# Two slots of query projection added ahead of a recurrence that keeps its slot number

## Chip, cores and metric

The kernel runs on one core of a Trainium2 chip. The metric is the device time of one execution in microseconds (us), the median of three runs. The core has five engines that run side by side, each through its own queue of instructions: TensorE (PE, matmuls, into the eight banks of PSUM), VectorE (DVE), ScalarE (ACT), GpSimd (POOL) and SyncE (SP, here the issuer of DMAs). They wait for one another by semaphores.

## What is computed

One step of a small streaming encoder layer in fp32, on 512 prompt tokens and 64 sample tokens (576 in all, 1024 wide). The part of the reference that the change touches:

```python
h = rmsnorm(x, norm1_g)
proj = h @ w_in
qa, ka, va, qb, fb, ib, gb = jnp.split(proj, [o1, o2, o3, o4, o5, o6], axis=-1)
att, k_new, v_new = swa_sink_attention(qa, ka, va, k_hist, v_hist, pos0, attn_sink)   # chunks of 64 queries
rec, s_new = hgrn2(qb, fb, ib, gb, lb, hgrn_norm_g, s0)
...
# hgrn2: per chunk, cum = cumsum(log f)
q_in = qf * jnp.exp(cum - ref);  k_in = kf * jnp.exp(ref - cum)
a = tril(q_in @ k_in.T);  o_intra = a @ vf
ds = (kf * jnp.exp(tot - cum)).T @ vf
...
o = (o_intra + o_inter), normed * norm_g * silu(g_in)
x = x + jnp.concatenate([att, rec], axis=-1) @ w_o
x = x + hier_moe(rmsnorm(x, norm2_g), ...);  final rmsnorm
```

The history of keys and the recurrent state are given for the sample tokens and zero for the prompt.

## The kernel before

Every engine's program is written out by hand in one function, with hand-placed semaphore waits. Tokens are cut into five tiles (four of 128, tile 4 with 64 rows), and chunks of 64 for the attention (NCHUNK = 9). fp32 products are made of three matmuls each over a high part and a low remainder of both operands; for weights, `high` (ACT) and `low` (DVE) make the two parts, and `splits` says in which slot. For tile 4 of the kinds f, i and g a projection (`halved`) packs the high and low part of the 64 tokens into one stationary operand, so it has 16 matmuls in place of 24; its two halves are added by `add_half` on DVE after ACT copied one of them.

The list `groups` gives the order of projections on PE: f (5 tiles), k and v (2 halves of the tokens each), q (4 head groups by 2 halves of 288 tokens), and then the fillers: i (5), b (8 halves, the recurrence's query), g (5: tile 4 first, then 0 to 3). Projection n writes PSUM bank n % 2 and waits till projection n - 2 has been emptied from it by `empty` on ACT or DVE.

After the first `first_filler` projections each engine walks over `slots`. In slot s PE makes the fill projections of the slot, then `scores(s)`, `turn_p(s - 1)` (transposes of the softmax) and `attend(s - 2)`; DVE makes `softmax_tail(s - 1)`, the emptying of the fill (or `add_half`), `softmax_head(s)`, `pt_with(s - 1)`, `take_o(s - 2)`; ACT makes the exponentials. POOL places q of a chunk into the block-diagonal operand `qbd`. The first step of the recurrence (tile 0) is tied to the slots by the constant EARLY = NCHUNK + 2 = 11: in slot 11 PE makes `decays(0)`, ACT `cum_exps(0)`, DVE a memset, the copies of k for the output (kout), `operands(0)` and `gain(0)` (which multiplies g of tile 0 by the norm's gain), and PE, behind the fill, `inner(0)`; in slot 12 DVE makes `inner_and_states(0)`, whose first operation is a masked copy of the scores, then `gain(1)`, and PE, behind the fill, `sums(0)`; in slot 13 DVE makes `normed(0)`. There are 14 slots, numbered from 0. The rest (recurrence of tiles 1 to 4 with the output projection w_o, router, experts) follows.

In the f stage x tiles are transposed by `turn_x(t)`, split by `h_high` (ACT) and `h_low` (DVE), and the squares for the norm are summed by `first_squares` on ACT.

Of the kernel before, what the change touches and what calls it, by code (L numbers as in the profile page):

```python
# [32 lines left out]
D = 1024  # L33
KC = D // P
# [4 lines left out]
CHUNK = 64  # L39
# [54 lines left out]
def program(nc, io):  # L94
    ctx = ExitStack()
    with ctx:
# [133 lines left out]
        oml = lb_bc[:, BW:2 * BW]  # L230
        kf_flat = kf[:, :, :].rearrange("p t k -> p (t k)")
        lb_t = kf_flat[:, 2 * BW:4 * BW]
        junk = kf_flat[:, 0:D]
        hT_flat = hT_f[:, :, :].rearrange("p k t -> p (k t)")
        s_flat = s_buf[:, :, :, :].rearrange("p a m k -> p (a m k)")
        vT = s_flat[:, 0:TOK]
        pt_flat = pt[:, 0, :, :].rearrange("p b k -> p (b k)")

        def hgrn_buffers(t):
# [128 lines left out]
            groups.append(("f", t, "act"))  # L368
        groups += [("k", 0, "dve"), ("k", 1, "dve")]
        groups += [("v", 0, "act"), ("v", 1, "act")]  # L370
        groups += [("q", i, "dve") for i in range(2 * GROUP)]
        first_filler = len(groups)
        groups += [("i", t, "act") for t in range(NT)]
        groups += [("b", i, "dve") for i in range(2 * BH)]
        groups += [("g", t, "act") for t in (NT - 1, 0, 1, 2, 3)]
# [11 lines left out]
        def wait_emptied(eng, kinds):  # L387

            for who, s in (("act", proj_act), ("dve", proj_dve)):
# [2 lines left out]
                    eng.wait_ge(s, max(last))  # L392


        slots = [[n] for n in of_kind["i"]] + [of_kind["b"][2 * m:2 * m + 2] for m in range(BH)] + \
                [[n] for n in of_kind["g"]]
        assert len(slots) >= NCHUNK + 2

# [31 lines left out]
        def h_lo(c):  # L430
            return (hT_lo_a, hT_lo_b)[c // (KC // 2)][:, c % (KC // 2), :]


        splits = {1: (4, 0, 4), 2: (4, 4, KC), 6: (5, 0, 4), 7: (5, 4, KC),

                  EARLY: (len(W_GROUPS), 0, 3), EARLY + 1: (len(W_GROUPS), 3, 6)}

        halved = [n for n, (kind, t, _) in enumerate(groups) if kind in "fig" and t == NT - 1]
        assert rows_of(NT - 1) == DEC and 2 * DEC == P
# [169 lines left out]
        def _(pool):  # L609
# [82 lines left out]
                      allow_small_or_imprecise_dtypes=True).then_inc(consts, 1)  # L692


            wait_emptied(pool, "q")
            for c in range(NCHUNK):
                if c >= 2:
                    pool.wait_ge(scores_ready, c - 1)
                for b in range(KV):
                    rows = slice(b * HD, (b + 1) * HD)  # L700
                    pool.tensor_copy(qbd[rows, c % 2, :, b * CHUNK:(b + 1) * CHUNK],  # L701
                                     qa[rows, :, c * CHUNK:(c + 1) * CHUNK]).then_inc(qbd_ready, 1)

                    pool.wait_ge(qbd_ready, KV * c + b + 1)
# [80 lines left out]
        def _(act):  # L785
# [63 lines left out]
            high(0, 4, KC)  # L849
            h_high(1)  # L850
            first_squares(1)
            h_high(2)
            first_squares(2)
            first_squares(3)
            act.wait_ge(lb_diff, 1)
            act.activation(lb_t[:, :], lb_t[:, :], ACT.Exp).then_inc(lb_exp, 1)
            first_squares(4)
            for n in range(first_filler):
                if groups[n][2] == "act":
                    empty(n)  # L860
                kind, index, _ = groups[n]
                if kind == "f" and index < 2:
                    h_high(3 + index)
                if (kind, index) == ("f", 2):
                    high(1, 0, KC)
                if kind == "v":
                    high(2, index * KC // 2, (index + 1) * KC // 2)
                if (kind, index) == ("q", 1):
                    act.wait_ge(v_turned, 1)
                    for tile in range(PROMPT_TILES):  # L870
                        act.activation(V[:, tile, :], ps[:, 7, tile * P:(tile + 1) * P], ACT.Copy,
                                       scale=stats[:, 3, tile:tile + 1]).then_inc(v_ready, 1)
                    act.activation(V[0:DEC, 5, :], ps[0:DEC, 6, 0:KVW], ACT.Copy,
                                   scale=stats[0:DEC, 3, NT - 1:NT]).then_inc(v_ready, 1)
                if (kind, index) == ("q", 5):
                    high(3, 0, KC)
                if groups[n][0] == "k" and groups[n][1] == 1:
                    for t in range(NT):
                        act.wait_ge(f_ready, t + 1)
                        act.activation(logf[0:rows_of(t), t, :], logf[0:rows_of(t), t, :], ACT.Ln).then_inc(logf_ready, 1)  # L880
# [39 lines left out]
                last.then_inc(osq_ready, 1)  # L920

            for s, fill in enumerate(slots):
                if s == NCHUNK:

                    wait_emptied(act, "b")
                    act.activation(qf[:, :, :], qf[:, :, :], ACT.Silu).then_inc(qf_ready, 1)
                if s == EARLY:
                    cum_exps(0)
                if s == EARLY + 2:
                    rec_squares(0)  # L930
                for n in fill:
                    if groups[n][2] == "act":
                        empty(n)
                if has_before(s - 1) and s - 1 < NCHUNK:
                    pt_before(s - 1)
                if s < NCHUNK:
                    exps(s)
                if s in splits:
                    high(*splits[s])
# [130 lines left out]
        def _(dve):  # L1070
# [321 lines left out]
            for s, fill in enumerate(slots):  # L1392
                if s == EARLY + 1:
                    inner_and_states(0)
                    gain(1)
                if s == EARLY + 2:
                    normed(0)
                if 1 <= s <= NCHUNK:
                    softmax_tail(s - 1)
                for n in fill:  # L1400
                    if groups[n][2] == "dve":
                        empty(n)
                    elif n in halved:
                        add_half(n)
                if s < NCHUNK:
                    softmax_head(s)
                if 1 <= s <= NCHUNK:
                    pt_with(s - 1)
                if 2 <= s < NCHUNK + 2:
                    take_o(s - 2)  # L1410
                if s == EARLY:
                    chain(dve.memset(hgrn_buffers(0)[3], 0.0))
                    dve.wait_ge(kout_turned, 1)
                    chain(dve.tensor_copy(kout[:, 0, :], ps[:, 6, 0:P]))
                    dve.tensor_copy(kout[0:DEC, 1, :], ps[0:DEC, 6, P:2 * P]).then_inc(kout_ready, 1)
                    operands(0)
                    gain(0)
                if s in splits:
                    low(*splits[s])
            chain(dve.memset(logits[:, :, :], 0.0))  # L1420
            def mix_low(t):
# [253 lines left out]
        def _(pe):  # L1675
# [8 lines left out]
                                        ident[0:r, 0:r])  # L1684
                last.then_inc(turned, 1)

            def project(n):

                kind, i, _ = groups[n]
                k = ring_of[kind]  # L1690
# [4 lines left out]
                b = n % 2  # L1695
                hi, lo = w_hi[k % RING], w_low(k)
                for c in range(KC):
                    if fresh:

                        pe.wait_ge(w_lo_done, KC * k + c + 1)  # L1700
                    if kind in "fig":
                        cols = slice(0, 512)
                        h_parts = (hT_hi[:, c, tok(i)], h_lo(c)[:, tok(i)])
                        w_parts = (hi[:, c, cols], lo[:, c, cols])
                        out = ps[0:rows_of(i), b, 0:cols.stop - cols.start]
                        stationary, moving = h_parts, w_parts
                    else:
                        m, half = ("kv".index(kind), i) if kind in "kv" else (i // 2, i % 2)
                        cols, toks = slice(m * P, (m + 1) * P), slice(half * HALF, (half + 1) * HALF)
                        stationary = (hi[:, c, cols], lo[:, c, cols])  # L1710
                        moving = (hT_hi[:, c, toks], h_lo(c)[:, toks])
                        out = bank(b, HALF)

                    if n in halved:
                        if c:
                            pe.matmul(out, hT_both[:, c, 0:DEC], moving[1], start=False, stop=False)
                        last = pe.matmul(ps[:, b, :], hT_both[:, c, :], moving[0], start=c == 0, stop=c == KC - 1)
                        if c == 0:
                            pe.matmul(out, hT_both[:, c, 0:DEC], moving[1], start=False, stop=False)
                        continue  # L1720
                    pe.matmul(out, stationary[0], moving[0], start=c == 0, stop=False)  # L1721
                    pe.matmul(out, stationary[0], moving[1], start=False, stop=False)  # L1722
                    last = pe.matmul(out, stationary[1], moving[0], start=False, stop=c == KC - 1)  # L1723
# [11 lines left out]
            stay_busy(8)  # L1735
            for t in range(NT):
                pe.wait_ge(hT_dve, t + 1)
                project(t)
                for following in ((1, 2), (3,), (4,), (), ())[t]:
                    turn_x(following)  # L1740

            pe.wait_ge(ck_in, 16)
            pe.wait_ge(hT_dve, NT)
# [146 lines left out]
            for s, fill in enumerate(slots):  # L1890
                if s == EARLY:

                    pe.wait_ge(o_taken, NCHUNK)
                    pe.transpose(ps[:, 6, 0:P], kT[:, SEQ - P:SEQ], ident[:, :])
                    pe.transpose(ps[0:DEC, 6, P:2 * P], kT[:, SEQ + WINDOW:], ident[:, :]).then_inc(kout_turned, 1)
                    decays(0)
                for n in fill:
                    project(n)
                if s < NCHUNK:
# [233 lines left out]
```

## Time and profile before

| | us |
|---|---|
| median of 3 runs | 532.94 (532.36 to 533.3) |
| the profiled execution, its own time | 531.83 |
| its span (first to last instruction) | 530.0 |
| PE busy | 477.0 (90%) |
| DVE busy | 335.2 (63%) |
| ACT busy | 231.0 (44%) |
| POOL busy | 104.8 (20%) |

The profile is of one execution. Busy shares are over the whole span; the stages have different limits. Times of rows are us from the start of the span.

### The profile page before, as it was taken

The numbers are of one execution on the slowest core, as the hardware profiler recorded it, in microseconds if no ns is written. First come the engines' busy times: TensorE is split into PE (matmuls) and PEld (weight loads), VectorE is DVE, ScalarE is ACT, GpSimd is POOL, SyncE is SP. The second block draws the span as 40 slices with busy tenths as digits, with TensorE's granted clock in tenths as the row PEclk, the third lists the DMA queues.
The fourth block names the chain that finished last, engine by engine and source line by source line (L and its number), as shares of the span: only waits on it lengthen the run. The fifth ranks groups of instructions, "written<-read, shape, count | busy, mean of one in ns | idle before, by whom it ended". The sixth has DMA issues, their size and how long they took to land.

```text
span 530.0 us, 7159 instructions
## 1 busy us (share of the span) xinstructions
PE 477.0 (90%) x2531; PEld 376.2 (71%) x2531; DVE 335.2 (63%) x659; ACT 231.0 (44%) x446; POOL 104.8 (20%) x168
## 2 busy tenths in 40 slices
PE   6899999899999999999998988899999999999400
PEld 5679898778896777678876877666766776677100
DVE  4786515676586357767563649697568657765176
ACT  6744712453355447224132234467266456544021
POOL 5481001101000000001001044021322322222143
PEclk9999999989999999999999868899999999999855
DMA  8804404004008500610110776999989989801295
GB/s 307 190 2 160 167 0 160 0 1 160 1 1 219 166 1 9 171 41 0 41 61 1 293 302 242 420 394 374 358 345 369 376 357 350 357 16 36 66 328 187
DMA packets 33100, 93.15 MB, mean 176 GB/s; under 512 B 10248, under 2 KB 13456, under 8 KB 26928
## 3 DMA queue, kind: packets, MB, share of 16 engines
q1 hardware_dynamic: 27728, 82.81, 43.3%
q0 software_dynamic: 5344, 9.97, 5.2%
q8 instruction: 17, 0.28, 0.2%
q14 instruction: 11, 0.09, 0.1%
HBM read 88.38 MB, written 13.89 MB: 193 GB/s over the span
## 4 chain that ended last, share of the span: by engine, by line
PE 75%; DVE 13%; ACT 5%; DMA 4%; issue 2%; SPq 1%; POOL 1%; POOLq 0%; ACTq 0%; DVEq 0%
PE ps L2053 10%; PE ps L1721 7%; PE ps L1723 6%; PE ps L1722 6%; PE ps L2072 6%; PE ps L2074 5%; PE ps L2073 5%; PE ps L1935 3%; PE ps L1937 3%; PE ps L1936 3%; DMA pair<-y_pairs 2%; PE ps L1959 2%; DVE gu_lo L1588 2%; DVE w_lo L1105 2%; PE ps L2034 2%
## 5 line engine op out<-in xcount | busy, mean ns | idle before, releaser
L1588 DVE TENSOR_TENSOR gu_lo<-we_gu,gu_hi 128x1024 fp32r<-128x1024 f32 x64 | 74.8, 1220 | 2.0 <-ACT gu_hi L1003 0.6
L1003 ACT ACTIVATE gu_hi<-we_gu 128x1024 fp32r<-128x1024 f32 x64 | 63.2, 1055 | 0.0
L2053 PE MATMUL ps<-we_d,hhT 128*128 128x512 f32 x128 | 56.9, 592 | 0.0
L2072 PE MATMUL ps<-gu_hi,xT_hi 128*128 128x512 f32 x128 | 52.9, 413 | 3.4 <-DVE xT_lo L1582 3.3
L2074 PE MATMUL ps<-gu_hi,xT_lo 128*128 128x512 f32 x128 | 50.9, 397 | 0.0
L2073 PE MATMUL ps<-gu_lo,xT_hi 128*128 128x512 f32 x128 | 50.4, 394 | 0.0
L1721 PE MATMUL ps<-hT_hi,w_hi 128*128 128x288 f32 x160 | 48.3, 302 | 0.6 <-DVE w_lo_q L1102 0.2
L1721 PE MATMUL ps<-w_hi,hT_hi 128*128 128x512 f32 x96 | 39.8, 414 | 2.4 <-DVE hT_lo_b L1088 1.1
L2053 PEld LDWEIGHTS ps<-we_d,hhT 128*128 128x128 f32 x128 | 23.4, 191 | 24.9 <-issue 24.9
L1722 PE MATMUL ps<-w_lo,hT_hi 128*128 128x512 f32 x96 | 38.0, 396 | 0.0
L1048 ACT ACTIVATE sg<-ps 128x256 f32<-128x256 f32 x16 | 6.1, 383 | 64.7 <-PE ps L2074 64.7
L1624 DVE TENSOR_TENSOR hh<-sg,ps 128x256 f32<-128x256 f32 x16 | 6.7, 421 | 41.3 <-ACT sg L1048 41.2
L1721 PEld LDWEIGHTS ps<-hT_hi,w_hi 128*128 128x128 f32 x160 | 30.1, 188 | 3.3 <-DVE w_lo_q L1102 1.7
L2072 PEld LDWEIGHTS ps<-gu_hi,xT_hi 128*128 128x128 f32 x128 | 24.5, 192 | 9.4 <-issue 2.5
L732 POOL DMA_INDIRECT y_pairs<-y,now_pair x12 | 13.9, 1162 | 79.8 <-DVE y L1617 78.0
L1105 DVE SCALAR_TENSOR_TENSOR w_lo<-ring,g_col,w_hi 128x512 fp32r<-128x512 f32 (+1 forms) x40 | 25.3, 697 | 7.0 <-ACT w_hi L815 7.0
L815 ACT ACTIVATE w_hi<-ring,g_col 128x512 fp32r<-128x512 f32 (+1 forms) x48 | 28.7, 681 | 0.6 <-DMA ring<-in_w_in 0.6
L1723 PE MATMUL ps<-hT_hi,w_lo 128*128 128x288 f32 x96 | 28.3, 295 | 0.0
L2073 PEld LDWEIGHTS ps<-gu_lo,xT_hi 128*128 128x128 f32 x128 | 24.5, 192 | 5.2 <-issue 0.5
L2074 PEld LDWEIGHTS ps<-gu_hi,xT_lo 128*128 128x128 f32 x128 | 24.3, 190 | 5.5
L701 POOL COPY qbd<-qa 64x256 f32<-64x256 f32 x18 | 7.2, 400 | 93.3 <-PE ps L1769 47.7
L1936 PE MATMUL ps<-w_lo,mix_hi 128*128 128x512 f32 x64 | 25.0, 390 | 0.0
(386 smaller groups left out, 1123.6 us busy)
## 6 DMA issues: line engine op xcount, KB each, us to landing
we_gu<-in_w_gate SPq DMA_DIRECT2D x16, 1024.0 KB, 7.8
we_gu<-in_w_up SPq DMA_DIRECT2D x16, 1024.0 KB, 11.1
we_d<-in_w_down SPq DMA_DIRECT2D x16, 1024.0 KB, 11.0
ring<-in_w_in SPq DMA_DIRECT2D x4, 2048.0 KB, 7.7
pair<-y_pairs SPq DMA_DIRECT2D x8, 512.0 KB, 7.8
ring<-in_w_in SPq DMA_DIRECT2D x3, 1024.0 KB, 8.0
x_first<-in_x_p SPq DMA_DIRECT2D x4, 512.0 KB, 9.6
x<-in_x_p SPq DMA_DIRECT2D x4, 512.0 KB, 4.0
```

The costliest lines, as they stand in the source:

```text
L815: act.activation(w_split(k, w_high(k, c)), w_raw(k, c), ACT.Copy, scale=gain).then_inc(w_hi_done, 1)
L1003: act.activation(gu_hi[slot % 2][:, :, 2 * q:2 * q + 2, :], we_gu[slot][:, :, 2 * q:2 * q + 2, :], ACT.Copy).then_inc(gu_hi_done, 1)
L1105: ins = dve.scalar_tensor_tensor(out, w_raw(k, c), g1_col[:, c:c + 1], hi, ALU.mult, ALU.subtract)
L1588: dve.tensor_tensor(gu_lo[slot][:, :, 2 * q:2 * q + 2, :], we_gu[slot][:, :, 2 * q:2 * q + 2, :], gu_hi[slot % 2][:, :, 2 * q:2 * q + 2, : ...
L1721: pe.matmul(out, stationary[0], moving[0], start=c == 0, stop=False)
L1722: pe.matmul(out, stationary[0], moving[1], start=False, stop=False)
L1723: last = pe.matmul(out, stationary[1], moving[0], start=False, stop=c == KC - 1)
L1936: pe.matmul(out, mix_hi[:, c, 0:r], w_l, start=False, stop=False)
L2053: last = pe.matmul(bank(4 + 2 * (slot % 2) + half), hhT[:, slot % 2, f, :], we_d[slot][:, f, 512 * half:512 * half + 512], start=f == 0, s ...
L2072: pe.matmul(bank(0), xT_hi[:, c, :], gu_h[:, :, c, :], start=c == 0, stop=False)
L2073: pe.matmul(bank(0), xT_hi[:, c, :], gu_l[:, :, c, :], start=False, stop=False)
L2074: last = pe.matmul(bank(0), xT_lo[:, c, :], gu_h[:, :, c, :], start=False, stop=c == KC - 1)
```

## The change

The second halves of the four q groups become fillers and form two new slots ahead of the others, so there are 16 slots: q, q, i x5, b x4 (two projections each), g x5. EARLY stays 11, so all five g are now in slots 11 to 15. Moved with them: the weight splits of slots 1, 2, 6, 7 go to 3, 4, 7, 8 with the low parts one slot later, behind `softmax_tail`; those of w_o go from EARLY, EARLY + 1 to EARLY + 2, EARLY + 3; the Silu of the recurrence's query moves from slot 9 to slot 10. POOL begins with chunk 0 when the first q halves are emptied. The x transposes stand inside the f projections, and the scratch of the squares (`junk`) moves to `s_buf`. `decays(0)` goes ahead of the wait for the last attention output and of the kout transposes.

```diff
@@ tables @@
-        groups += [("q", i, "dve") for i in range(2 * GROUP)]
+        groups += [("q", 2 * m, "dve") for m in range(GROUP)]
         first_filler = len(groups)
+        groups += [("q", 2 * m + 1, "dve") for m in range(GROUP)]
         groups += [("i", t, "act") for t in range(NT)]
...
-        slots = [[n] for n in of_kind["i"]] + [of_kind["b"][2 * m:2 * m + 2] for m in range(BH)] + \
+        late_q = of_kind["q"][GROUP:]
+        slots = [late_q[0:2], late_q[2:4]] + [[n] for n in of_kind["i"]] + [of_kind["b"][2 * m:2 * m + 2] for m in range(BH)] + \
                 [[n] for n in of_kind["g"]]
...
-        splits = {1: (4, 0, 4), 2: (4, 4, KC), 6: (5, 0, 4), 7: (5, 4, KC),
+        splits = {3: (4, 0, 4), 4: (4, 4, KC), 7: (5, 0, 4), 8: (5, 4, KC),
...
-                  EARLY: (len(W_GROUPS), 0, 3), EARLY + 1: (len(W_GROUPS), 3, 6)}
+                  EARLY + 2: (len(W_GROUPS), 0, 3), EARLY + 3: (len(W_GROUPS), 3, 6)}
@@ POOL @@
-            wait_emptied(pool, "q")
             for c in range(NCHUNK):
+                if c == 0:
+                    pool.wait_ge(proj_dve, emptied[of_kind["q"][GROUP - 1]][1])
+                if c == HALF // CHUNK:
+                    wait_emptied(pool, "q")
@@ ACT @@
             h_high(1)
             first_squares(1)
-            h_high(2)
             first_squares(2)
-            first_squares(3)
             act.wait_ge(lb_diff, 1)
             act.activation(lb_t[:, :], lb_t[:, :], ACT.Exp).then_inc(lb_exp, 1)
-            first_squares(4)
+            h_high(2)
...
                     h_high(3 + index)
+                    first_squares(3 + index)
...
-                if s == NCHUNK:
+                if s == EARLY - 1:
@@ DVE @@
                 if 1 <= s <= NCHUNK:
                     softmax_tail(s - 1)
+                    if s - 1 in splits:
+                        low(*splits[s - 1])
...
-                if s in splits:
+                if s in splits and s >= EARLY:
                     low(*splits[s])
@@ PE @@
-            def project(n):
+            def project(n, following=None):
...
+                    if c == (2 if n else 5) and following is not None:
+                        turn_x(following)
...
-                project(t)
-                for following in ((1, 2), (3,), (4,), (), ())[t]:
-                    turn_x(following)
+                project(t, t + 1 if t < NT - 1 else None)
...
+                    decays(0)
                     pe.wait_ge(o_taken, NCHUNK)
                     pe.transpose(ps[:, 6, 0:P], kT[:, SEQ - P:SEQ], ident[:, :])
                     pe.transpose(ps[0:DEC, 6, P:2 * P], kT[:, SEQ + WINDOW:], ident[:, :]).then_inc(kout_turned, 1)
-                    decays(0)
```

The order of instructions shows it at three places. First DVE at the first slots that split weights, before (line L1105 makes the low parts, L1213 to L1216 are the softmax tail of chunk 1, L1198 the next softmax head):

```order
L1205 TENSOR_TENSOR small<-sink_bc,small 128x4
L1225 COPY pt<-ps 64x512
L1105 SCALAR_TENSOR_TENSOR w_lo_105<-ring,g_col,w_hi_86 128x512 x4
L1213 TENSOR_TENSOR small<-small 128x4
L1214 RECIPROCAL small<-small 128x4
L1216 TENSOR_SCALAR s_buf<-s_buf,small 128x128 x4
L1198 TENSOR_TENSOR s_buf<-ps,bias 128x4x192
```

and after, where DVE first splits weights in a slot (the same lines are L1109, L1217 to L1220 and L1202 there):

```order
L1229 COPY pt<-ps 64x512
L1233 COPY mixT<-ps 128x4x64
L1217 TENSOR_TENSOR small<-small 128x4
L1218 RECIPROCAL small<-small 128x4
L1220 TENSOR_SCALAR s_buf<-s_buf,small 128x192 x4
L1109 SCALAR_TENSOR_TENSOR w_lo_105<-ring,g_col,w_hi_86 128x512 x4
L1202 TENSOR_TENSOR s_buf<-ps,bias 128x4x192
```

The low parts stood ahead of a softmax tail and now stand behind one, three chunks later.

Second, DVE in slots 9 to 12, before (the row of gg with 64 rows is `add_half` of g's tile 4; L1412 to L1415 are memset and kout copies, L1247 to L1257 `operands(0)`, L1238 `gain`, L1277 the masked copy):

```order
L1133 TENSOR_TENSOR gg<-gg,ps 64x512
L1225 COPY pt<-ps 64x512
L1229 COPY mixT<-ps 128x4x64 x2
L1412 MEMSET pt 128x512
L1414 COPY kout<-ps 128x128
...
L1247 TENSOR_TENSOR s_buf<-s_buf,qf 128x512
L1249 TENSOR_TENSOR s_buf<-s_buf,ps 128x512
...
L1238 TENSOR_TENSOR gg<-gg,ng_bc 128x512
L1107 TENSOR_TENSOR w_lo_105<-ring,wo_hi_top 128x512 x2
L1107 TENSOR_TENSOR w_lo_105<-ring,wo_hi_q 128x512
L1277 COPY_PREDICATED pt<-causal,ps 128x512
```

and after, from slot 10 on:

```order
L1229 COPY pt<-ps 64x512
...
L1233 COPY mixT<-ps 128x4x64
L1137 TENSOR_TENSOR gg<-gg,ps 64x512
L1418 MEMSET pt 128x512
L1420 COPY kout<-ps 128x128
...
L1251 TENSOR_TENSOR s_buf<-s_buf,qf 128x512
L1253 TENSOR_TENSOR s_buf<-s_buf,ps 128x512
...
L1242 TENSOR_TENSOR gg<-gg,ng_bc 128x512
L1281 COPY_PREDICATED pt<-causal,ps 128x512
```

The addition of the half tile moved from ahead of the last attention copies to directly ahead of the memset, and between gain(0) and the masked copy no weights are split.

Third, PE from the last attention matmuls to `inner(0)`, before (L1894 and L1895 are the kout transposes, L1827 to L1834 the decays, L1721 to L1723 a full projection of 24 matmuls, L1851 the start of `inner(0)`):

```order
L1809 MATMUL ps<-pt,V 64x256 x2
L1894 MATMUL ps<-ident,kT 128x128
L1895 MATMUL ps<-ident,kT 64x128
L1827 MATMUL ps<-decay_m,logf 128x256
L1832 MATMUL ps<-ident,kf 128x128
...
L1834 MATMUL ps<-logf,tail_m 128x512
L1721 MATMUL ps<-w_hi_87,hT_hi 128x512
L1722 MATMUL ps<-w_lo_106,hT_hi 128x512
...
L1723 MATMUL ps<-w_hi_87,hT_lo_b 128x512
L1851 MATMUL ps<-s_buf 128x128 x4
```

and after (L1724 to L1727 are the halved projection of 16 matmuls):

```order
L1815 MATMUL ps<-pt,V 64x256 x2
L1833 MATMUL ps<-decay_m,logf 128x256
L1838 MATMUL ps<-ident,kf 128x128
...
L1840 MATMUL ps<-logf,tail_m 128x512
L1901 MATMUL ps<-ident,kT 128x128
L1902 MATMUL ps<-ident,kT 64x128
L1725 MATMUL ps<-w_hi_87,hT_both 128x512
L1727 MATMUL ps<-w_lo_106,hT_both 64x512
...
L1725 MATMUL ps<-w_hi_87,hT_both 128x512
L1857 MATMUL ps<-s_buf 128x128 x4
```

The decays come first, and the projection between them and `inner(0)` is the halved one.

## Rows read from the trace of the kernel before

**Rows 1.** The page: busy us and share of the span; chain by engine.

```profile
PE 477.0 (90%) x2531; PEld 376.2 (71%) x2531; DVE 335.2 (63%) x659; ACT 231.0 (44%) x446; POOL 104.8 (20%) x168
...
PE 75%; DVE 13%; ACT 5%; DMA 4%; issue 2%; SPq 1%; POOL 1%; POOLq 0%; ACTq 0%; DVEq 0%
```

**Rows 2.** Timeline, PE, f projections: start, us, line, count, [idle before, releaser].

```profile
18.15 0.50 PE L1721 MATMUL ps<-w_hi,hT_hi 128*128 128x512 f32 x1 [1.14 <-DVE hT_lo_b L1088]
...
23.77 1.04 PE L1683 MATMUL ps<-ident,x_first 128*128 128x128 f32 x8
25.68 0.47 PE L1721 MATMUL ps<-w_hi,hT_hi 128*128 128x512 f32 x1 [0.87 <-ACT logf L836]
```

**Rows 3.** Timeline, DVE, ACT and PE, end of f and second half of k.

```profile
43.83 0.67 DVE L1133 TENSOR_TENSOR logf<-logf,ps 64x512 f32<-64x512 f32 x1
...
44.53 0.72 ACT L830 ACTIVATE logf<-logf,stats 64x512 f32<-64x512 f32 x1 [2.53 <-DVE logf L1133]
...
45.88 0.29 PE L1721 MATMUL ps<-hT_hi,w_hi 128*128 128x288 f32 x1
```

**Rows 4.** Timeline, DVE and PE, third slot.

```profile
100.70 2.74 DVE L1105 SCALAR_TENSOR_TENSOR w_lo<-ring,g_col,w_hi 128x512 fp32r<-128x512 f32 x4 [1.84 <-ACT w_hi L815]
...
104.84 0.66 PE L1785 MATMUL ps<-ident,s_buf 128*128 128x128 f32 x4 [1.39 <-DVE s_buf L1216]
```

**Rows 5.** Windows, PE: stretch, its us, PE busy, granted clock, DMA share, GB/s.

```profile
105.00:107.00 2.00, 2.00 (x12) 0.91 0.03 8
107.00:110.00 3.00, 3.00 (x9) 0.50 0.00 0
...
308.00:321.00 13.00, 13.00 (x64) 0.50 0.52 201
...
324.00:326.00 2.00, 0.23 (x3) 1.00 0.93 287
...
332.00:334.00 2.00, 0.70 (x7) 1.00 1.02 422
...
335.00:338.00 3.00, 3.00 (x9) 0.56 1.01 418
```

**Rows 6.** Timeline, PE, from slot 9 to inner(0).

```profile
167.98 0.65 PE L1806 MATMUL ps<-pt,V 64*64 64x256 f32 x4
...
176.57 0.33 PE L1894 MATMUL ps<-ident,kT 128*128 128x128 f32 x1 [0.53 <-DVE mixT L1229]
...
185.37 1.05 PE L1851 MATMUL ps<-s_buf 128*128 128x128 f32 x8
```

**Rows 7.** Timeline, DVE, slots 9 to 12.

```profile
169.54 0.68 DVE L1133 TENSOR_TENSOR gg<-gg,ps 64x512 f32<-64x512 f32 x1 [2.63 <-ACT gg L827]
170.14 0.68 DVE L1225 COPY pt<-ps 64x512 f32<-64x512 f32 x1
...
176.57 0.48 DVE L1412 MEMSET pt<- 128x512 f32 x1
...
177.44 0.28 DVE L1415 COPY kout<-ps 64x128 f32<-64x128 f32 x1
180.72 0.69 DVE L1247 TENSOR_TENSOR s_buf<-s_buf,qf 128x512 f32<-128x512 f32 x1 [2.99 <-ACT s_buf L906]
...
182.73 0.68 DVE L1257 TENSOR_TENSOR s_buf<-s_buf,kf 128x512 f32<-128x512 f32 x1
...
188.62 0.73 DVE L1277 COPY_PREDICATED pt<-causal,ps 128x512 f32<-128x512 int32 x1
```

**Rows 8.** Timeline, ACT, slots 9 to 11.

```profile
168.91 0.59 ACT L827 ACTIVATE gg<-ps 64x512 f32<-64x512 f32 x1
...
185.57 0.69 ACT L842 ACTIVATE gg<-ps,stats 128x512 f32<-128x512 f32 x1 [2.11 <-PE ps L1723]
```

**Rows 9.** Timeline, PE, first and last matmul of g's half tile, slot 9.

```profile
162.84 0.51 PE L1717 MATMUL ps<-w_hi,hT_both 128*128 128x512 f32 x1
...
166.42 0.40 PE L1717 MATMUL ps<-w_hi,hT_both 128*128 128x512 f32 x1
```

More of the change, by code:

```diff
@@ L232, in program @@
         lb_t = kf_flat[:, 2 * BW:4 * BW]
-        junk = kf_flat[:, 0:D]
         hT_flat = hT_f[:, :, :].rearrange("p k t -> p (k t)")
@@ L236, in program @@
         vT = s_flat[:, 0:TOK]
+        junk = s_flat[:, 0:D]
         pt_flat = pt[:, 0, :, :].rearrange("p b k -> p (b k)")
@@ L867, in _ @@
                     high(2, index * KC // 2, (index + 1) * KC // 2)
-                if (kind, index) == ("q", 1):
+                if (kind, index) == ("q", 2):
                     act.wait_ge(v_turned, 1)
@@ L874, in _ @@
                                    scale=stats[0:DEC, 3, NT - 1:NT]).then_inc(v_ready, 1)
-                if (kind, index) == ("q", 5):
+                if (kind, index) == ("q", 4):
                     high(3, 0, KC)
```

## The prediction, before the changed kernel ran

> **What bounds the kernel now.** I read the page first: its busy shares and the chain of work that ended last. TensorE (PE) is busy for 477.0 of 530.0 us and holds 75% of the chain [rows 1]. So a change of order can only win where PE stands idle or runs at its lower clock, and it loses wherever it makes PE wait anew. No matmul is added or removed. Next came PE's timeline, stage by stage, for its idle times up to the recurrence; then the clock granted around them; then, for the slots whose content changes, the timelines of VectorE (DVE) and ScalarE (ACT), to see how long their chains between two pieces of PE work are.
>
> PE's idle times that the change touches are four. In the f projections PE waits 1.14 us before f of tile 1 and 0.87 us before f of tile 2 [rows 2]: the transposes of the next x tile run after a projection, and their split on ACT and DVE stands uncovered. In the third slot it waits 1.39 us for the softmax of chunk 1, because DVE made four low parts of weights first, 100.70 to 103.44 [rows 4]. Some 2 us after PE resumed, the granted clock was 0.50 for 3 us [rows 5]. Before the transposes of k for the output it waits 0.53 us for the last attention copy [rows 6].
>
> **The change, part by part: what is won.**
>
> Transposes inside the f projections. They cover both waits, 1.14 + 0.87 = 2.0 us. The projections then arrive 2.0 us earlier at k, but k's second half writes the PSUM bank that held f of the half tile 4. That bank is given free by a chain over DVE (the addition at 43.83) and ACT (the sigmoid from 44.53, ended 45.25), and PE began this half at 45.88 [rows 3]. DVE reaches the addition only 0.6 us earlier than now: its queue up to there follows the x transposes of tile 4, which lose the idle 2.0 us ahead of them but get two of the eight chunks of f3 there, 2 x 0.7 = 1.4 (a full projection takes 18.15 to 23.77, 5.6 us [rows 2]). PE would be at k's half at 45.88 - 2.0 = 43.9 and may go at 45.25 - 0.6 = 44.7, so 0.8 us comes back as a new wait. **Won: 1.2 us**; bounds 0.6 (nothing but DVE's own gain) and 2.0 (all).
>
> Query halves as fill of slots 0 and 1, low parts behind the softmax tail. In the slot that waits, no weights are split any more, and where they are split (slots 4, 5, 8, 9) the four low parts stand behind the scaling of the probabilities. That scaling comes 2.74 us earlier than behind the low parts, twice the 1.39 us that PE waited. **Won: 1.4 us**, and with it the stretch at half clock: 3 us at 0.50 and 2 us at 0.91 make 1.5 + 0.2 = **1.7 us** [rows 5]. The two extra slots cost PE nothing by themselves: the same eight query halves are projected. Their emptying on DVE stands in slots without low parts. SP's loads of the next weights hang on the last query and b projections, which stand where they stood in the sum of PE's work; the first need is slots later. POOL's four reciprocal-root pairs come some us later, ahead of mask work that nobody asks for before the first softmax.
>
> decays(0) ahead of the k transposes: covers the wait of 0.53 us. **Won: 0.5 us.** Together 1.2 + 1.4 + 1.7 + 0.5 = **4.8 us**.
>
> **What is lost.** It is in slots 11 and 12, where the number EARLY stayed 11 while the slots moved by two.
>
> Slot 11. Before, its fill was the g projection of tile 1, and add_half for the half tile 4 had been done in slot 9. Now the fill is tile 4 itself. Two things follow. The fill is short: 162.84 to 166.8, 3.9 us [rows 9], where a full one takes 5.6 [rows 2]. And DVE's queue has add_half in front of the memset, the two kout copies and the five operations of operands(0). It can't start before PE has ended the fill and ACT has copied the half, and inner(0) on PE waits for all of it. From the fill's end: 0.05 to ACT; the copy starts and 0.63 later the addition (168.91 [rows 8] to 169.54 [rows 7]); 0.60 to the next DVE operation (169.54 to 170.14); memset to second kout copy 176.57 to 177.72, 1.15; operands(0) 180.72 to 183.41, 2.69 [rows 7]; some 0.1 for the hops. That is **5.2 us of idle PE** in place of none: today inner(0) starts at 185.37 without a wait [rows 6], with operands(0) over at 183.41. ACT's exponentials don't lengthen it: the last of operands(0), which reads the last of them, began at 182.73 [rows 7], and after the change they run under the short fill.
>
> Here a rule bears. Today the copy of transposed probabilities at 170.14 stood behind the addition at 169.54, though PE had gone on to the next work at 167.98 [rows 6, 7]: DVE did not overtake its waiting head. The Trainium skill, "TensorE: Matmul & The Clock Gate", in the section on the array's architecture, says that ScalarE's and VectorE's queues are strictly first in, first out, and the trace agrees. If DVE could overtake, operands(0) would be done under the fill, nothing of the 5.2 would be left, and the sum would be 532.0 instead of 537.2. I go by the row.
>
> Slot 12. gain(0) is still issued in slot 11 and waits for the g projection of tile 0, which is now slot 12's own fill. Behind it in DVE's queue is the masked copy of the scores, and sums(0) on PE waits for that. From the end of the fill: ACT's Silu 0.69 (as at 185.57 [rows 8]), gain 0.60 (its 0.69 less the overlap with the next), the masked copy 0.73 (as at 188.62 [rows 7]), three hops 0.15: **2.2 us**. Today this DVE work was over while PE still had fill. gain(1) waits in the same manner for slot 13's fill, but what is queued behind it (normed(0), low parts of w_o) is needed only after slot 15, two projections later: nothing.
>
> The clock. After the idle 1.39 us, and after one of 1.45 us around 333, the granted clock was half for about 3 us; after the idle around 306 it was half for 13 us; after 1.8 us in 324 to 326 it did not fall [rows 5]. A wait of 5.2 us is longer than any of them, so I count one fall of the common size, **1.7 us**. The wait of 2.2 us follows some 9 us later; the row nearest in length, and soon after a half-clock stretch, is that of 324 to 326, without a fall: I count 0, and 1.7 as the other bound.
>
> Together 5.2 + 2.2 + 1.7 = **9.1 us**.
>
> **The sum.** +9.1 - 4.8 = +4.3. The profiled execution took 531.83 (its span of 530.0 and 1.8 around it), which gives 536.1. The median of the runs shown is 532.94, 1.1 more than the profiled one: 537.2. Everything after slot 15 is PE work whose waits are relative to it, so the shift is carried to the end.
>
> **Rivals.**
>
> Two falls of the clock, or a long one. For it: three of the four idle times in [rows 5] were followed by half clock, and 2.2 us is more than each. +1.7: 538.9. Chance 0.22.
>
> No fall at all, or all 2.0 us of the f stage won: 535.5 or 536.4, both 534.7. 0.08.
>
> The softmax wait comes back where low parts now stand (slots 4 and 5). ACT and DVE then do high and low parts between two softmaxes, and PE has some 9 us a slot. Against it: the tail is ahead of them. If it came, the 1.4 and 1.7 wouldn't be won: 540.3. 0.05.
>
> The other side: the recurrence doesn't wait. If DVE's chain were covered in both slots and the clock kept, -4.8 would be left: 528.1. It decides where the two waits with their clock cost are under 4.8 together. For it: I place ACT and DVE by rows of other slots, and some of the 5.2 could be done ahead. Against: all eight operations stand behind add_half in the order. 0.08.
>
> The shift moves the clock elsewhere. The router stage ran at half clock from 308 to 321 [rows 5]. If this stretch were 3 us as the others, (13 - 3)/2 = 5 us would be won: 532.2, and if gone, 530.7. For it: a fall is not tied to one place. Against: the idle time before it, and all its order, stay. 0.10: 0.04 of it faster than before, 0.06 the same.
>
> **How the numbers follow.** The forecast's own case (one fall) has 0.47 and lies within 536 to 538.2. The range of 8 in 10 takes in no fall with the full win (534.7) and two falls (538.9) with 0.5 around: 534.2 to 539.4. A measurement of this kernel tells 0.2%, 1.1 us, from no change. Faster: 0.08 + 0.04 = 0.12; the same 0.06; slower the rest, 0.82.
>
> **What the profile after would show.** Right: no idle at the third slot's probability transposes and full clock behind it; under 0.2 us at the k transposes; PE idle 4.5 to 5.8 us before the first s_buf matmul of inner(0), released by DVE, with the DVE row of gg (64 rows) directly ahead of the memset; PE idle about 2.2 before the first pt/vf matmul of sums(0), released by the DVE masked copy; half clock for about 3 us behind the first; f stage idle under 0.3 and a new short wait before k's second half. Wrong: if inner(0) is released at once, or if the attention slots show new waits of over 1 us. The forecast fails if the clock after the waits behaves otherwise, above all in the router stage.

## The result, and the profile after

The changed kernel takes 539.12 us (median of 4 runs, 538.01 to 541.44); the kernel before took 533.08 on the same chip. The ratio is 1.0121, with a 95% interval of 1.0082 to 1.0161: slower by 6.0 us, where +4.3 was predicted. The profiled executions are 8.3 us apart (540.14 against 531.83): that of before lies 1.2 under its median, that of after 1.0 above. Experiments are compared by their ratios, and their parts by positions in the profiled executions.

The page of the kernel after, with busy time and the chain by engine, as in [rows 1]:

```profile
PE 480.7 (89%) x2531; PEld 379.0 (70%) x2531; DVE 336.3 (62%) x659; ACT 231.4 (43%) x446; POOL 108.7 (20%) x168
...
PE 78%; DVE 10%; issue 4%; ACT 3%; DMA 3%; POOL 1%; SPq 0%; POOLq 0%; ACTq 0%; DVEq 0%
```

PE issues the same 2531 matmuls and is busy 3.7 us longer for them. More idle time alone would not do that: more of the same work ran at the lower clock. The page can't say where; the timeline and the windows can. This is the timeline of PE of the kernel after (start, us, line, tiles, count, idle time before and who ended it), around the two slots of the recurrence:

```profile
169.10 0.39 PE L1725 MATMUL ps<-w_hi,hT_both 128*128 128x512 f32 x1
174.77 2.05 PE L1857 MATMUL ps<-s_buf 128*128 128x128 f32 x8 [5.28 <-DVE s_buf L1261]
...
187.42 0.46 PE L1881 MATMUL ps<-vf,pt 128*128 128x128 f32 x2 [2.80 <-DVE kT L1294]
```

Before, inner(0) [rows 6] and sums(0) started without a wait. This is the first matmul of sums(0) there, and the window of both slots (stretch, its us, PE busy, granted clock, DMA share, GB/s):

```profile
193.02 0.38 PE L1875 MATMUL ps<-vf,pt 128*128 128x128 f32 x2
```

```profile
165.00:196.00 31.00, 30.34 (x160) 1.00 0.50 136
```

What they now wait for stands in the timelines of DVE and ACT of the kernel after, which answer to [rows 7, 8]:

```profile
169.53 0.59 ACT L832 ACTIVATE gg<-ps 64x512 f32<-64x512 f32 x1 [1.85 <-PE ps L1725]
...
170.15 0.68 DVE L1137 TENSOR_TENSOR gg<-gg,ps 64x512 f32<-64x512 f32 x1 [7.34 <-ACT gg L832]
170.89 0.48 DVE L1418 MEMSET pt<- 128x512 f32 x1
...
173.94 0.69 DVE L1261 TENSOR_TENSOR s_buf<-s_buf,kf 128x512 f32<-128x512 f32 x1
...
185.38 0.69 DVE L1242 TENSOR_TENSOR gg<-gg,ng_bc 128x512 f32<-128x512 f32 x1 [10.75 <-ACT gg L847]
185.99 0.72 DVE L1281 COPY_PREDICATED pt<-causal,ps 128x512 f32<-128x512 int32 x1
186.60 0.68 DVE L1294 COPY kT<-ps 128x512 f32<-128x512 f32 x1
```

DVE stands idle for 7.34 us with the addition of the g half at its head. The memset, the two copies of k for the output and operands(0), which need nothing of that fill, stand behind it, and PE waits for the last of them. In the next slot the gain stands at the head for 10.75 us. Behind it stand the masked copy and, which the prediction had not counted, the copy of the first chunk's state into kT.

The windows of the kernel after, in the same columns:

```profile
169.00:172.00 3.00, 0.49 (x3) 1.00 1.08 322
172.00:173.00 1.00, 0.00 (x0) 0.59 1.06 211
173.00:179.00 6.00, 4.23 (x25) 0.50 1.06 311
179.00:180.00 1.00, 1.00 (x5) 0.99 1.00 361
180.00:189.00 9.00, 6.20 (x30) 1.00 0.06 17
189.00:190.00 1.00, 1.00 (x5) 0.63 0.00 0
190.00:196.00 6.00, 6.00 (x16) 0.50 0.01 3
196.00:197.00 1.00, 1.00 (x6) 0.96 0.00 0
...
292.00:295.00 3.00, 3.00 (x8) 0.50 0.00 0
...
319.00:329.00 10.00, 10.00 (x50) 0.50 0.54 211
```

Each of the two waits has a stretch at 1.2 GHz (granted clock 0.50) beside it. Where a window is part full and part half clock, its mean tells where the level changed: 0.59 in 172 to 173 puts the first fall at 172.2. It begins inside the wait itself and lasts to 179.0. The second begins some 2 us after the wait has ended, at 189.3, with PE fully busy, and lasts to 196.1. Each is 6.8 us long. Before, the clock was full through both slots.

The order of the losses is best seen by one marker that both kernels have, the transposes of rec(0)'s result. They start at 201.63 before and at 210.06 after: +8.43. The next such marker, of rec(1), is at +8.44 (222.60 and 231.04), and the end at +8.3. So all of the difference is made in the first 210 us. Behind it, a further half-clock stretch at 291 to 295 adds 1.6 and the stages behind that give 1.7 back.

### The profile page after: what moved, and what is told of

Same layout as the page of the kernel before. It is cut to its first block, busy times and chain, and to the rows that moved or that the text cites. A ratio compares the mean times of both kernels' runs of the same rounds, so it can differ in the third digit from the quotient of the medians.

```text
span 538.3 us, 7159 instructions
## 1 busy us (share of the span) xinstructions
PE 480.7 (89%) x2531; PEld 379.0 (70%) x2531; DVE 336.3 (62%) x659; ACT 231.4 (43%) x446; POOL 108.7 (20%) x168
## 4 chain that ended last, share of the span: by engine, by line
PE 78%; DVE 10%; issue 4%; ACT 3%; DMA 3%; POOL 1%; SPq 0%; POOLq 0%; ACTq 0%; DVEq 0%
PE ps L2059 10%; PE ps L1729 8%; PE ps L1731 7%; PE ps L1730 7%; PE ps L2078 5%; PE ps L2080 5%; PE ps L2079 5%; PE ps L1941 3%; PE ps L1942 3%; PE ps L1943 3%; PE ps L1775 2%; PE ps L1965 2%; DMA pair<-y_pairs 2%; PE ps L1881 1%; PE ps L2040 1%
## 5 line engine op out<-in xcount | busy, mean ns | idle before, releaser
L1109 DVE SCALAR_TENSOR_TENSOR w_lo<-ring,g_col,w_hi 128x512 fp32r<-128x512 f32 (+1 forms) x40 | 25.9, 712 | 0.0
```

The lines of the kernel that those rows point to most:

```text
L1109: ins = dve.scalar_tensor_tensor(out, w_raw(k, c), g1_col[:, c:c + 1], hi, ALU.mult, ALU.subtract)
```

## The experiments

Two theories stood against each other. **Queue:** the loss is DVE's first-in-first-out order, which puts work that PE needs behind work that waits for PE's own fill; mend the order and the waits and both falls of the clock go. **Place:** the loss comes with the recurrence starting two slots nearer to its operands, or from a clock that falls wherever the program happens to stand. Beside these stood a question of size: what a fall of the clock costs. All edits are to the kernel after, except the two that say before.

**The half tile of g is not the fill in front of the recurrence (e1_g_order).** The tile of 64 rows goes to slot 13, and a full one, whose result DVE need not add up, to slot 11.

```diff
-        groups += [("g", t, "act") for t in (NT - 1, 0, 1, 2, 3)]
+        groups += [("g", t, "act") for t in (0, 1, NT - 1, 2, 3)]
```

> The changed kernel with one edit: the order of g is tile 0, 1, half tile 4, 2, 3 instead of 4, 0, 1, 2, 3. Queue theory (VectorE's order makes the waits: the addition of the half tile ahead of operands(0), and gain(0) ahead of the masked copy while g of tile 0 is still to be projected): slot 11 holds a full fill and no addition, slot 12's gain(0) finds g of tile 0 emptied. Both waits of TensorE (5.28 and 2.80 us) fall to under 0.3 us, the stretches at half clock at 172 to 179 and 189 to 196 are gone, about 13 us less than the changed kernel: 526 to 528, some 5 us faster than the kernel before. Rival (the early slots don't leave ScalarE time for the moved Silu and the exponentials of the recurrence): waits of 1 us or more stay before inner(0), time above 530.

Measured: 528.78 us (8 runs), ratio to before 0.9928 [0.9904, 0.9952]. Both waits are gone. The windows of this kernel:

```profile
170.00:180.00 10.00, 10.00 (x61) 1.00 1.07 288
180.00:196.00 16.00, 16.00 (x72) 1.00 0.09 31
...
257.00:260.00 3.00, 3.00 (x8) 0.55 0.00 0
```

The recurrence still begins in slot 11, so Place is refuted: with another order of five tiles the change is faster than before by 0.7%. The last row was not expected: a fall with PE busy throughout.

**One head of the queue at a time (e2_add_behind, e3_gain_behind).** The first puts the addition behind operands(0), the second moves the gain behind inner_and_states(0).

```diff
-                    elif n in halved:
+                    elif n in halved and s != EARLY:
                         add_half(n)
...
                     operands(0)
+                    add_half(fill[0])
                     gain(0)
```

> The changed kernel with the addition of the half tile in slot 11 behind operands(0), ahead of gain(0). Queue theory: operands(0) ends some 169.0, before the short fill ends at 169.5; the wait before inner(0) goes from 5.28 to under 0.3 us, with the fall of the clock behind it; the wait of 2.80 before sums(0) stays, and one stretch at half clock may follow it: 5.3 + 2 = 7 us less than the changed kernel, 531 to 534. Rival (the fill of 16 matmuls is too short for the chain from decays over exponentials to operands, whoever stands first in the queue): a wait of 1.5 us or more stays, 534 to 536.

Measured: 533.77 us (10 runs), 1.0009 [0.998, 1.0038]. In the timeline of DVE of this kernel operands(0) now ends under the fill, and the addition follows:

```profile
168.61 0.68 DVE L1261 TENSOR_TENSOR s_buf<-s_buf,kf 128x512 f32<-128x512 f32 x1
...
170.35 0.68 DVE L1137 TENSOR_TENSOR gg<-gg,ps 64x512 f32<-64x512 f32 x1 [1.05 <-ACT gg L832]
```

and inner(0) starts at 169.52 without a wait. The wait of slot 12 stays at 2.80. Its windows:

```profile
170.00:178.00 8.00, 7.37 (x46) 1.00 1.06 278
178.00:180.00 2.00, 0.00 (x0) 0.93 1.06 400
180.00:189.00 9.00, 8.82 (x24) 0.50 0.11 35
```

The wait of 2.80 alone, at full clock until then, brings a stretch of 10.2 us at 1.2 GHz, from 179.7, which is inside the wait, to 189.9; PE worked in 9.8 us of it. From the first matmul of decays(0) to the marker this kernel takes 41.58 us, and 34.17 with e1's order; less the wait of 2.80, 4.6 is left as the price of that one stretch.

```diff
                     inner_and_states(0)
+                    gain(0)
                     gain(1)
...
                     operands(0)
-                    gain(0)
```

> The changed kernel with gain(0) issued behind the masked copy and the states of tile 0 instead of ahead of them. Queue theory: the wait before sums(0) goes from 2.80 to 0, the wait of 5.28 before inner(0) stays, with the half clock that begins in it (about 2 us); the second half-clock stretch is gone if the wait of 2.80 brought it: 2.8 + 2.9 = 5 to 6 us less than the changed kernel, 533 to 535. Rival (the second fall of the clock belongs to the first wait and its late echo): the wait goes but the second half-clock stretch stays, 536 to 537.

Measured: 536.0 us (7 runs), 1.0047 [1.0017, 1.0078]. The wait of 5.28 stays and that of slot 12 is gone:

```profile
174.00:180.00 6.00, 4.89 (x26) 0.50 1.06 292
181.00:204.00 23.00, 23.00 (x106) 1.00 0.04 12
```

With the second wait its fall is gone too, so the half clock of 190 to 196 hangs on the wait of 2.80 and is no late part of the first. The same stretch takes 42.07 here: less 5.28 and e1's 34.17, 2.6 for the first fall.

**Both heads moved (e4_both_behind): the two edits together.**

> The changed kernel with both edits of e2_add_behind and e3_gain_behind, EARLY still 11 and g's order unchanged. Queue theory: the short fill of the half tile in slot 11 is no harm by itself; both waits are gone and with them both stretches at half clock, from decays(0) to the transposes of turn_rec(0) 34.2 us as in e1_g_order (47.8 in the changed kernel), time 527 to 529. Rival (the two stand-alone edits did not add up because the short fill leaves PE early at sums(0) or inner(0)): a wait of 0.5 us or more at one of them, 529 to 531.

Measured: 528.86 us (10 runs), 0.9938 [0.9911, 0.9965]; 34.21 for the stretch, e1's 34.17 within the reading. Two ways to free DVE's queue, one by the order of tiles and one by the order of DVE's own work, give the same time. In the router stage this execution ran some of the time at full clock, where before it ran at half [rows 5]. The waits of PE and the windows there:

```profile
PE ps L2041 <- DMA xg<-h_rows,table_tok: 5.5, 1, 5.5
```

```profile
302.00:309.00 7.00, 6.19 (x55) 1.00 1.01 411
316.00:320.00 4.00, 0.30 (x2) 0.53 0.36 94
```

PE was early and then stood 5.5 us for the gathered rows. From the stage's first transposes to the first expert matmul it took 20.10 us, against 18.94 before with 13 us at half clock. The execution of e5 below shows it more plainly: full clock in this stage till PE stood 7.0 us for the same rows, and 19.98 us in all. So in these two executions more full clock won nothing there, and the rival that wanted 5 us from it had the wrong limit. Why the rows came some 1.5 us later after the stage's start than before is not shown.

**The same waits, with PE kept busy in them (e5_kept_busy, f4_busy_less).** Behind the two fills PE multiplies the identity into an unused bank; the work of the reference is all done, and this is added. The first kernel had 40 and 20 such matmuls, the second 22 and 11 (the trace has two records for each):

```diff
                     project(n)
+                if s == EARLY:
+                    stay_busy(22)
+                if s == EARLY + 1:
+                    stay_busy(11, 3)
```

> The changed kernel with idle matmuls (128 by 128 on the identity, results unused) after the fills of slots 11 and 12, 40 and 20 of them, so that TensorE works while it would wait. Clock theory: both waits stay in length (VectorE's chain is as long) but the clock stays at full, and about 5 us of the 13 come back: 534 to 535, and the spread between executions (538.0 to 541.4) shrinks. Rival (the clock falls by itself in this stage, whatever TensorE does, as it did at 107 in the kernel before): no change, 538 to 540.

> The changed kernel with 22 and 11 idle matmuls behind the fills of slots 11 and 12 instead of the 40 and 20 that took 8.9 and 4.4 us and so outlasted the waits by 3.5 and 1.6 us (a matmul of this kind took 0.22 us). Clock theory: 22 take 4.9 and 11 take 2.4 us, they fit into the waits of 5.28 and 2.80 us, TensorE starts inner(0) and sums(0) when it does in the changed kernel, but at full clock: from the decays to the last transposes of slot 15's successor 47.8 - 5 = 42 to 43 us, time 534 to 536. Rival (the clock falls by length of the stage, not by idle time): half clock again between 172 and 196, 538 to 540.

Measured: 541.83 us (4 runs), 1.0162 [1.012, 1.0204] for the first. Its 40 matmuls took 8.9 us and its 20 took 4.4, and outlasted the waits by 3.5 and 1.5 us. Yet the stretch from decays(0) to the marker took 47.61 against 47.79: the full clock gave back what the overshoot took. The rest of its time over the kernel after comes behind the marker, from one short stretch at half clock more and from the router stage:

```profile
PE ps L2044 <- DMA xg<-h_rows,table_tok: 7.0, 1, 7.0
```

Overshoot and clock are one sum of two unknowns, so the second kernel was sized to the waits: 536.41 us (10 runs), 1.0065 [1.0036, 1.0095]. Its timeline, and its windows:

```profile
169.34 5.07 PE L1737 MATMUL ps<-ident 128*128 128x128 f32 x44
174.79 0.46 PE L1857 MATMUL ps<-s_buf 128*128 128x128 f32 x2 [0.37 <-DVE s_buf L1261]
...
182.53 2.62 PE L1737 MATMUL ps<-ident 128*128 128x128 f32 x22
185.50 0.46 PE L1881 MATMUL ps<-vf,pt 128*128 128x128 f32 x2 [0.35 <-DVE kT L1294]
```

```profile
173.00:179.00 6.00, 5.63 (x46) 1.00 1.06 307
190.00:196.00 6.00, 6.00 (x29) 1.00 0.00 0
```

inner(0) starts at 174.79, where it starts at 174.77 in the kernel after: the wait is as long, only filled, and so is the second. From inner(0) to sums(0) it takes 10.71 us instead of 12.65, and from there to the marker 19.55 instead of 22.64. The marker is at 205.05 instead of 210.06. The two falls by themselves cost 5.0 us, 1.9 the first and 3.1 the second, and nothing but the clock differs.

**The parts that win, each alone (f1_low_behind, f2_turns_inside, of before).** f1 has the low parts behind softmax_tail, one slot later; f2 has the f stage of the change and nothing else.

```diff
                     softmax_tail(s - 1)
+                    if s - 1 in splits:
+                        low(*splits[s - 1])
...
-                if s in splits:
+                if s in splits and s >= EARLY:
                     low(*splits[s])
```

> The kernel before with one part of the change alone: the low parts of the weights in slots 1, 2, 6, 7 one slot later, behind the softmax tail. Nothing else moves, the attention begins where it did. Order theory (the third slot's wait of 1.39 us and the half clock behind it come from the low parts ahead of the tail, not from where the attention begins): both go, 1.4 + 1.7 = 3.1 us less than the kernel before, up to where the clock falls elsewhere. Rival (in slots with i as fill the softmax chain of ScalarE and VectorE is too long in any order, and only the two slots with query halves take the pressure off): the wait stays or appears in slot 3, less than 1 us won.

Measured: 531.1 us (10 runs), 0.9957 [0.9927, 0.9987]. The wait of [rows 4] and the half clock behind it [rows 5] are gone, and a new wait has come two slots later:

```profile
119.20 0.33 PE L1786 MATMUL ps<-ident,s_buf 128*128 128x128 f32 x1 [0.74 <-DVE s_buf L1216]
```

From scores(0) to the first matmul of decays(0) it takes 85.84 us against 88.06, so 2.2 won of the 3.1 that the wait and its clock were put at; the new wait is most of the rest.

```diff
                 for c in range(KC):
+                    if c == (2 if n else 5) and following is not None:
+                        turn_x(following)
...
-                for following in ((1, 2), (3,), (4,), (), ())[t]:
-                    turn_x(following)
+                project(t, t + 1 if t < NT - 1 else None)
```

> The kernel before with the f stage of the change alone: the x transposes inside the f projections, ScalarE's order of squares and splits, the scratch in s_buf. Theory: the waits of 1.14 and 0.87 us go, one of 1.23 us comes before the second half of k, as in the changed kernel: 0.8 to 1.0 us earlier from q on, about 0.9 us less in time. Rival (the whole stage is paced by VectorE's chain of low parts, so the shift is eaten up before q): no shift at q, no difference.

Measured: 532.05 us (10 runs), 0.999 [0.996, 1.0019]: 0.7 us at the q transposes, no more than the times can tell. It shows what such a new wait has to do with the clock. The timeline of PE, and a window of it:

```profile
104.18 0.66 PE L1784 MATMUL ps<-ident,s_buf 128*128 128x128 f32 x4 [1.40 <-DVE s_buf L1215]
...
113.77 0.33 PE L1783 MATMUL ps<-ident,s_buf 128*128 128x128 f32 x1 [1.39 <-DVE s_buf L1215]
```

```profile
107.00:110.00 3.00, 3.00 (x15) 1.00 0.00 0
```

Here the wait of 1.40 is not followed by half clock, and one of 1.39 stands a slot later, where the slowed PE of before had none. The stretch from scores(0) to decays(0) takes 88.06 us, exactly as before. So a slow PE had hidden a wait, and the fall there was worth about nothing while DVE was late in the next slot as well.

**The recurrence two slots later (f3_early_13), and the best version (b2_best13).** In f3 the recurrence starts in slot 13 with the two low parts of w_o where they were relative to it; slot numbers have grown by two, so it begins in the same work as before.

```diff
-EARLY = NCHUNK + 2
+EARLY = NCHUNK + 4
...
-                  EARLY + 2: (len(W_GROUPS), 0, 3), EARLY + 3: (len(W_GROUPS), 3, 6)}
+                  EARLY: (len(W_GROUPS), 0, 3), EARLY + 1: (len(W_GROUPS), 3, 6)}
```

> The changed kernel with EARLY = 13 in place of 11 (w_o's splits stay in slots 13 and 14): the recurrence moves with the slots, as in the kernel before, two of the five g are done before it. Slot theory (the loss is that EARLY stayed): inner(0) and sums(0) wait for nothing, no half clock there, as in e1_g_order: 527 to 530. Rival (a rest of the loss is in the early attention itself, as the Silu and the exponentials of the recurrence now meet): waits of 1 us or more at inner(0) stay.

Measured: 527.19 us (4 runs), 0.9893 [0.9833, 0.9953]. The marker is at 196.48, 5.15 ahead of before: this is the winning half of the change with nothing lost.

b2 also puts the addition of the f half in DVE's queue ahead of gate_f(3). It was the same kind of fault in small: in the kernel after, the second half of k waits for it.

```profile
44.88 0.40 PE L1729 MATMUL ps<-hT_hi,w_hi 128*128 128x288 f32 x1 [1.23 <-ACT logf L835]
```

```diff
             gate_f(2)
-            gate_f(3)
             add_half(halved[0])
+            gate_f(3)
```

> f3_early_13 with one more edit: the addition of f's half tile on VectorE goes ahead of gate_f(3), 1.8 us earlier, since k's second half waits 1.23 us for the bank that it frees. Bank theory: this wait goes, q comes 0.5 to 1.2 us earlier, time 526.0 to 527. Rival (q is paced by VectorE's chain up to the low parts of q's weights, which is as long): the wait goes, the shift at q is under 0.3 us, no difference to f3_early_13. Both are faster than the kernel before by about 1%.

Measured: 526.33 us (6 runs), 0.9887 [0.9847, 0.9927]. The 1.23 is gone and the q transposes come 1.16 earlier than in f3, 58.42 for 59.58, and the marker at 195.33 for 196.48. It is the fastest version here, 1.1% under before; its distance to f3 is told by the positions, not by the intervals, which overlap.

## Why the prediction was right and wrong, point by point

- **The winning side, predicted 4.8:** f3 has it alone, 5.15 at the marker. The f stage gave 0.9 where 1.2 was put: k's second half waits 1.23, where 0.8 was put, for DVE's addition starts 0.4 earlier (43.41 in the kernel after) and not 0.6. The remaining 4.2 came in the attention and at the k transposes, where 3.6 was put (1.4 and 1.7 for the third slot, 0.5 for k). All three went as forecast: f3's PE has no idle time and full clock from the q transposes to the marker. Another 0.14 is a small wait of before that went as well, and some 0.5 is not placed. What the prediction had not seen is that the low parts' order alone doesn't give the 3.1: by f1 it is 2.2, for a new wait comes two slots on, and by f2 a full clock alone gives nothing, for a wait comes in the next slot. In f3 and in the kernel after neither slot has a wait. Their first two slots have halves of q as fill; that this is why was not tested alone.
- **Slot 11, predicted 5.2:** 5.28, by the path that was described (ACT's copy, the addition, eight operations behind it). e2 shows the cause: with operands(0) ahead of the addition there is no wait. The Trainium skill, "TensorE: Matmul & The Clock Gate", in the section on the array's architecture, has VectorE's queue strictly first in, first out; the trace agrees, with DVE idle for 7.34 us while ready work stood behind its head.
- **Slot 12, predicted 2.2:** 2.80. The term stopped at the masked copy. PE's first sums also need the state of the first chunk, and that copy stands one place further back in the same queue: 186.60 after 185.99, 0.6 more. What PE waits for last was read off the order of before, in which neither was late.
- **The clock, predicted one fall of 1.7: this is the step that failed.** It read "I count one fall of the common size" for the wait of 5.2, and of the wait of 2.2 "I count 0". There were two falls, and f4 puts them at 5.0 together, 1.9 and 3.1. The count was wrong because a single row of 1.8 us of idle without a fall was taken for the nearest case; e2 and e3 show that the wait of 2.80 brings one whether the other was there or not. That row was a weak guide: at the same place in f4, with as long a wait, the clock did fall (below). The size was wrong because 3 us at half clock was taken as the common length: these stretches lasted 6.8 us each, and 10.2 in e2. Half of the time that PE worked in them comes near their price: 2.1 for the first, of which only 4.2 us were work, and 3.4 for the second, 5.5 by that reading against the 5.0 measured. The rival with two falls (538.9, chance 0.22) named what came but had the second at 1.7. That it lies within 0.2 us of the median is luck: its loss of 10.8 stands against 13.6 at the marker, and the medians happen to be 2.3 us nearer to one another than the profiled executions.
- **The sum.** At the marker the kernel after is 13.6 us behind f3: 5.28 + 2.80 + 5.0 = 13.1, with 0.5 not placed. Against f3's -5.15 that is +8.43, the measured shift. The prediction had 9.1 for 13.6 and 4.8 for 5.15. In medians the difference is 6.0 and not 8.3; I took the profiled span as standing 1.1 under the median for both kernels, and for the kernel after it stood 1.0 above.
- **Other rivals.** The softmax wait did not come back in slots 4 and 5. The recurrence did wait. The router stage kept a long stretch at half clock and would have had nothing to give (e4).

## What to carry to other kernels

Before work for the matmul engine is moved, write down for each vector engine what stands in its queue behind every operation that waits for the moved work, and ask of each of those who waits for it: a 0.7 us addition at the head of DVE's queue cost PE 5.28 us and, with the clock, 7.9 (42.07 of e3 against e1's 34.17). The cure was an order, of tiles (e1) or of three lines (e4), and each makes of a change that loses 1.2% one that wins 0.6 to 0.7%. Price a wait of the lengths seen here ahead of dense matmuls at its length and a clock fall besides: 3.1 to 4.6 us for the waits of 2.8, 1.9 to 2.6 us for those of 5.3. And test an expected gain from the clock by asking whether the next vector engine could keep up with the faster PE.

## What the runs showed of the hardware that was not expected

- A wait's length does not tell by itself whether the clock falls. After 1.39 us of idle it fell [rows 4, 5], after 1.40 in f2 at the same place it did not, and after 1.8 it did not [rows 5]. After 2.80 it fell in the kernel after and in e2. The 1.8 us before the first expert matmul shows the same: no fall behind it before [rows 5], and one at once in f4, where PE had also waited 1.33 us shortly ahead of it:

```profile
332.47 0.76 PE L2082 MATMUL ps<-gu_hi,xT_hi 128*128 128x512 f32 x1 [1.83 <-DVE xT_lo L1588]
```

```profile
333.00:336.00 3.00, 3.00 (x9) 0.51 1.02 422
```

- It can fall with PE busy for long: to 0.55 at 257 to 260 in e1, while f3 has the same three microseconds at 1.00; and to 0.50 at 292 to 295 in the kernel after. f3 has its own at 278. Every profiled execution but that of before has such a stretch of 3.4 us, starting at 238.8 in f1 at the earliest and at 294.1 in e5 at the latest, with next to no idle time ahead of it; e5, f1 and f4 have two. No run here shows why. They may be part of the spread of runs of one kernel (538.0 to 541.4 for the kernel after); that was not tested. They are no rival for the two falls of slots 11 and 12: in the nine executions where both waits are absent or filled, the clock stayed full from 110 to 238 us.
- A half-clock stretch lasted 3.4, 6.8, 10.2 and 13.7 us in different places; nothing in the rows before it told which.
- Matmuls of the identity that nobody reads (0.22 us each) kept the clock at 1.00 through a wait of 5.28 us and gave back 5.0 us. Where the wait can be removed, that is worth more: a ratio to before of 0.9928 (e1) or 0.9938 (e4) against 1.0065.
